# Window attention in a two-layer encoder: both halves of the 64-column values in one stationary tile, and weight splits moved to GpSimd

## The chip, the cores and the metric

The kernel runs on one core of a Trainium2 chip. The metric is the device time of one execution in microseconds (us), the median of several runs; less is better.

## What is computed

A trunk of two layers is applied to two independent groups (prompt and sample) of 512 tokens with 1024 features. Layer 0 uses latent attention with 8 heads, layer 1 uses windowed attention: 16 query heads of 64 columns share 2 key/value heads, a query block of 128 tokens sees its own and the two neighbouring key blocks, and each head adds a slope bias and a sink to its softmax. Both layers also attend into 256 memory tokens, multiply the branches by a gate, and project back. The part of the reference that the change touches is this one:

```python
def swa_mixer(q, k, v, q_norm, k_norm, sink):
    ...
    def attend(args):
        i, q_blk = args
        start = i * BLOCK
        k_blk = lax.dynamic_slice_in_dim(kp, start, 3 * BLOCK, axis=1)
        v_blk = lax.dynamic_slice_in_dim(vp, start, 3 * BLOCK, axis=1)
        ...
        s = jnp.einsum('bqkgd,bjkd->bkgqj', q_blk, k_blk).astype(jnp.float32) * scale
        s = jnp.where(valid, s - slopes * dist, NEG)
        sk = jnp.broadcast_to(sink_l, s.shape[:-1] + (1,))
        p = jax.nn.softmax(jnp.concatenate([s, sk], axis=-1), axis=-1)[..., :-1]
        return jnp.einsum('bkgqj,bjkd->bqkgd', p.astype(v_blk.dtype), v_blk)
...
branch = jnp.concatenate([mix, mem_o], axis=-1) * jax.nn.silu(gate)
x = x + branch @ p['w_out'][i]
```

## The kernel before, in words

**Precision.** Each fp32 operand of a matrix product is split into a high half (a copy in the type fp32r) and a low half (the value minus the high half, again fp32r). A product is then three matmuls: high x high, high x low, low x high (`mm3`, lines 1509 to 1511). ScalarE makes the high half with a copy, VectorE the low one with a subtraction. For weights that is `w_hi_to` (line 553) and `w_lo_to` (line 881); for a PSUM bank it is `hi` (line 560) and `lo` (lines 889 and 891). GpSimd splits only four weight tiles in the whole program (line 1368).

**Stages.** The program runs four layers in a row: L = 0 and 1 for the first group, 2 and 3 for the second. Odd L are the window layers. In one of them there are, in order: memory values and keys, projections of the tokens, memory attention, keys and values of the window part (`bKV`), queries (`bQ`), then a loop over the 16 heads, here called the window stage, and the output projection (`out`). The results of `bKV` for the values go to the tile `v0` (printed as `v` in the trace): for each key block k and each of the two value heads, 64 columns, written twice side by side, so that the 128 rows of the product hold the output in the lower and again in the upper 64 partitions; `v0[:, 0]` has the high, `v0[:, 1]` the low half.

**The loop over the heads.** Every engine has its own list of instructions, written by hand, and the engines meet at semaphores. In iteration h:

- TensorE: scores of head h+2 (`b_s`), one "fill" tile, on even h the transposes of a later query pair (`b_q`), the product with the values of head h (`b_o`), one or two more fill tiles, the transposes of the probabilities of head h+1 (`b_pt`). A fill tile is a weight row block of 256 columns from another projection (late queries, gates, parts of the output projection); `WINDOW_FILL` says how many stand before and after `b_o`.
- VectorE: low half of the weights for the first fill (`w_lo_to`), bias, row maximum of head h+2 (`b_max`, lines 1270 and 1274), low half of the queries on even h, the multiplication of `b_o`'s bank by the gate (`gated`, line 942), low halves of the weights for the second fills, sum and reciprocal of head h+2 (lines 985 and 987), low half of the transposed probabilities of head h+1 (`b_pt`, line 889). Where a chunk of fill tiles ends, its bank is also added to the residual (line 969) or to the gate (line 936) on the way.
- ScalarE: high half of the weights for the first fill, of the queries on even h, exponentials of head h+2 (lines 820 and 578), high halves of the weights for the second fills, of the transposed probabilities of head h+1, and from h = 8 on a branch split (line 591).
- GpSimd: probabilities of head h+2 times the reciprocal (line 1393, four instructions), in the first four heads the scaling of the late queries (lines 1339, 1340, 1486), and the low half of finished branches (line 1373).

The heads work two ahead, so the scores of head h+2 are computed while head h is finished. A weight tile's low half is needed by TensorE about four tiles later. PSUM has 8 banks; `plan()` hands them out ahead of time by a small model of how long each use lasts (`BANK_USE`), and a use waits until the one before it in the same bank has been read. That table's numbers set no order of the work, only which bank is taken.

`b_o` in the kernel before, for each of the four key blocks (two see 384 query columns, two 256):

```python
ins = mm3(bank(use)[:, lo_q * P:(hi_q + 1) * P],
          tuple(v0[:, a, k, c * P:(c + 1) * P] for a in range(2)),
          tuple(windowT[h % 2][:, a, SHARED_FROM[s] + col:SHARED_FROM[s] + col + span(k)]
                for a in range(2)), k == order[0], k == order[-1], skip=True)
```

## Time and profile before

| | us |
|---|---|
| median of 3 runs (lowest, highest) | 1433.49 (1433.2, 1434.6) |
| the profiled execution, its time | 1434.05 |
| the profiled execution, its span in the trace | 1432.3 |
| busy in the span: TensorE matmuls | 1393.2 (97%) |
| busy: VectorE, ScalarE, GpSimd | 981.5, 760.0, 412.8 (69%, 53%, 29%) |
| granted TensorE clock | 0.999 of full speed |

The profiled execution's own time is 0.6 us above the median of the runs and 1.75 us above its span, so times worked out on the span can be carried over to the runs by differences. The window stage takes place twice, from about 559 to 688 us and from about 1268 to 1397 us of the span. Busy shares of TensorE count overlapping matmuls as one stretch. In the rows, a name such as `w_lo_t<-w_raw,w_hi` says what an instruction writes and reads, `x2` that two instructions were merged into one row, and the bracket at a row's end how long the engine had been idle and who released it.

### The profile page before, as it was taken

Reading aid. Unit: us, or ns where it says so; the run is one execution under the profiler, and the core shown is the slowest. Engines: PE = TensorE matmul, PEld = TensorE weight load, DVE = VectorE, ACT = ScalarE, POOL = GpSimd, SP = SyncE. Lnnn points to the kernel's source line nnn. Section 1 sums busy time; section 2 is a strip of 40 time slices with the busy share of each in tenths; the row PEclk is TensorE's granted clock in tenths of the full one; section 3 lists DMA queues with packets and bytes.
Section 4 is the critical chain, followed back from the end, with each engine's and each line's share of the span. In section 5 each row is a group of like instructions: output and inputs, shape, how many; then the busy total and the mean of one; then the engine's idle time right before and its main releaser. Section 6 shows DMA issues by size and latency. Waiting matters only on the chain.

```text
span 1432.3 us, 23084 instructions
## 1 busy us (share of the span) xinstructions
PE 1393.2 (97%) x8120; PEld 1236.3 (86%) x8120; DVE 981.5 (69%) x2072; ACT 760.0 (53%) x1823; POOL 412.8 (29%) x535
## 2 busy tenths in 40 slices
PE   7999999999999999999999999999999999998999
PEld 6889889898888888798888898899888888887997
DVE  6555687887655647888664656888877556578883
ACT  7354466555544436666463535656655345366661
POOL 2231252330202223734212213422311112246450
PEclk9999999999999999999999999999999999999999
DMA  6413221114341222222262132121133413122222
GB/s 224 119 49 88 77 69 46 43 50 146 118 133 55 78 71 82 62 65 90 96 198 82 50 94 79 51 62 47 38 103 126 121 49 96 58 77 60 67 71 103
DMA packets 88674, 121.47 MB, mean 85 GB/s; under 512 B 10353, under 2 KB 58865, under 8 KB 88561
## 3 DMA queue, kind: packets, MB, share of 16 engines
q1 hardware_dynamic: 83088, 112.31, 25.9%
q10 hardware_dynamic: 5472, 7.69, 1.8%
q8 instruction: 66, 1.08, 0.3%
q14 instruction: 48, 0.39, 0.1%
HBM read 115.77 MB, written 4.19 MB: 84 GB/s over the span
## 4 chain that ended last, share of the span: by engine, by line
PE 72%; DVE 12%; ACT 9%; issue 4%; POOL 2%; ACTq 1%; DMA 0%; SPq 0%; DVEq 0%; POOLq 0%
PE bank L1509 22%; PE bank L1511 21%; PE bank L1510 21%; PE bank L1555 5%; ACT prob L578 4%; DVE bank L1270 3%; DVE w_lo_t L881 3%; DVE probT L889 2%; POOL rr L1340 1%; ACT w_hi L553 1%; PE bank L1515 1%; PE bank L1516 1%; ACT q_st L575 1%; DVE nmax L1274 1%; POOL rtmp L1339 1%
## 5 line engine op out<-in xcount | busy, mean ns | idle before, releaser
L881 DVE TENSOR_TENSOR w_lo_t<-w_raw,w_hi 128x256 fp32r<-128x256 f32 (+3 forms) x540 | 302.1, 575 | 288.4 <-ACT w_hi L553 276.0
L553 ACT ACTIVATE w_hi<-w_raw 128x256 fp32r<-128x256 f32 (+3 forms) x544 | 268.5, 509 | 334.3 <-PE bank L1511 310.2
L1509 PE MATMUL bank<-w_hi,actT 128*128 128x256 f32 (+3 forms) x1120 | 361.5, 323 | 5.5 <-DVE probT L889 3.4
L1510 PE MATMUL bank<-w_lo_t,actT 128*128 128x256 f32 (+3 forms) x1120 | 359.1, 321 | 0.0
L1509 PEld LDWEIGHTS bank<-w_hi,actT 128*128 128x128 f32 x1120 | 212.5, 190 | 21.7 <-DVE w_lo_t L881 5.6
L1510 PEld LDWEIGHTS bank<-w_lo_t,actT 128*128 128x128 f32 x1120 | 212.6, 190 | 14.3
L1393 POOL TENSOR_TENSOR prob<-prob,rinv 128x256 f32<-128x256 f32 x192 | 137.9, 748 | 283.7 <-DVE rinv L987 283.7
L1511 PE MATMUL bank<-w_hi,brlo 128*128 128x256 f32 (+1 forms) x608 | 189.0, 311 | 0.0
L578 ACT ACTIVATE prob<-bank,nmax 128x256 f32<-128x256 f32 (+2 forms) x256 | 138.3, 551 | 79.3 <-DVE nmax L1181 39.7
L1511 PE MATMUL bank<-w_hi,actT 128*128 128x512 f32 (+3 forms) x512 | 170.1, 332 | 0.0
L1509 PE MATMUL bank<-actT,w_hi 128*128 128x512 f32 x384 | 152.8, 398 | 3.9 <-DVE probT L889 2.3
L1510 PE MATMUL bank<-actT,w_hi 128*128 128x512 f32 x384 | 150.0, 391 | 0.0
L1511 PE MATMUL bank<-actT,w_lo_t 128*128 128x512 f32 x384 | 150.0, 391 | 0.0
L1339 POOL TENSOR_SCALAR rtmp<-ss 128x4 f32<-128x4 f32 (+2 forms) x84 | 25.2, 300 | 394.1 <-DVE ss L901 301.8
L1511 PEld LDWEIGHTS bank<-w_hi,brlo 128*128 128x128 f32 x608 | 115.7, 190 | 6.3
L889 DVE TENSOR_TENSOR probT<-bank,probT 128x512 fp32r<-128x512 f32 (+1 forms) x192 | 111.4, 635 | 8.3 <-ACT probT L560 7.3
L560 ACT ACTIVATE probT<-bank 128x512 fp32r<-128x512 f32 (+1 forms) x192 | 95.1, 573 | 39.2 <-PE bank L1555 39.2
L1373 POOL TENSOR_TENSOR brlo<-gate,actT 128x512 fp32r<-128x512 f32 x48 | 63.7, 1334 | 180.4 <-ACT actT L591 180.4
L1511 PEld LDWEIGHTS bank<-w_hi,actT 128*128 128x128 f32 x512 | 96.8, 189 | 7.5
L1555 PE MATMUL bank<-ident,prob 128*128 128x128 f32 x704 | 90.7, 275 | 9.1 <-ACT prob L578 6.5
L1340 POOL TENSOR_TENSOR rr<-rtmp,mhalf 128x4 f32<-128x4 f32 (+2 forms) x84 | 93.6, 1114 | 7.0
L1555 PEld LDWEIGHTS bank<-ident,prob 128*128 128x128 f32 x704 | 78.3, 140 | 18.7 <-ACT prob L578 8.6
(141 smaller groups left out, 2710.7 us busy)
## 6 DMA issues: line engine op xcount, KB each, us to landing
w_raw<-in_w_mem SPq DMA_DIRECT2D x64, 256.0 KB, 2.6
w_raw<-in_w_out SPq DMA_DIRECT2D x112, 128.0 KB, 2.1
w_raw<-in_w_b SPq DMA_DIRECT2D x112, 128.0 KB, 2.1
w_raw<-in_w_b SPq DMA_DIRECT2D x48, 256.0 KB, 2.7
w_raw<-in_w_out SPq DMA_DIRECT2D x40, 256.0 KB, 2.8
w_raw<-in_w_a SPq DMA_DIRECT2D x32, 256.0 KB, 2.7
w_raw<-in_w_a SPq DMA_DIRECT2D x64, 128.0 KB, 2.0
bias<-in_alibi ACTq DMA_DIRECT2D x28, 192.0 KB, 2.3
```

The source lines that it names most:

```text
L553: act.activation(w_hi[:, n % SPLIT, 0:width], w_raw[:, n % RAW, 0:width], ACT.Copy).then_inc(w_hi_done, 1)
L560: act.activation(out, in_, ACT.Copy, scale=1.0 if gain is None else gain).then_inc(hi_done, 1)
L578: ins = act.activation(out, in_, ACT.Exp, bias=nmax[:, par, c:c + 1], accum_out=psumx[:, par, c:c + 1])
L881: dve.tensor_tensor(w_lo_t[:, n % SPLIT, 0:width], w_raw[:, n % RAW, 0:width], w_hi[:, n % SPLIT, 0:width].bitcast(fp32), ALU.subtract).th ...
L889: ins = dve.tensor_tensor(out, in_, hi_part, ALU.subtract)
L1340: nc.gpsimd.tensor_tensor(dst, rtmp[:, 0:n], mhalf[:, 0:n], ALU.pow).then_inc(signal, 1)
L1373: nc.gpsimd.tensor_tensor(brlo[:, j, :], gate[:, j, :], actT[:, j, :].bitcast(fp32), ALU.subtract).then_inc(br_lo, 1)
L1393: pool.tensor_tensor(t, t, rinv[:, par, i:i + 1].to_broadcast(list(t.shape)), ALU.mult).then_inc(p_pool, 1)
L1509: nc.tensor.matmul(out, lhs[0], rhs[0], start=start, stop=False, skip_group_check=skip)
L1510: nc.tensor.matmul(out, lhs[0], rhs[1], start=False, stop=False, skip_group_check=skip)
L1511: return nc.tensor.matmul(out, lhs[1], rhs[0], start=False, stop=stop, skip_group_check=skip)
L1555: ins = nc.tensor.transpose(bank(use)[:, c * P:(c + 1) * P], src, ident[:])
```

## The change

**Values.** `v0[:, 0]` now holds for each value head 64 columns of the high half followed by 64 columns of the low half. The copy of ScalarE and the subtraction of VectorE write 128 x 2 x 64 elements per token block, where each wrote 128 x 256 before. `b_o` needs two matmuls per key block, with the high and with the low half of the probabilities as the moving operand, and leaves the high values' product in the lower 64 rows of the bank and the low values' product in the upper 64. A product low x low is thereby added, which was left out before.

**Adding the halves.** ScalarE copies the upper 64 rows times 0.5 to a tile `o_low` in partitions 0 to 63 (`b_low`, ahead of the exponentials of head h+2). VectorE adds the lower rows times 0.5 and writes to the lower or upper half of `o_pair` (`b_sum`, in the place of `gated`). On odd heads GpSimd multiplies the gate by the pair (`gate_pair`), after the probabilities of head h+2. The branch split of ScalarE waits for that (`o_gated`), and on even heads `b_sum` waits until GpSimd has read the pair before. Both new tiles lie where `v0[:, 1]` has no use in the window stage.

**Weight splits.** The low halves of the 256-column tiles whose place is the second fill of an iteration (`late_split`) go from VectorE to GpSimd, ahead of the probabilities of head h+2: 23 tiles in each window stage, 46 in all. Heads 0 to 3 and 6 to 10 have two such tiles each, heads 4, 5 and 11 to 13 have one.

**Planner.** `bO` counts 1.18 in place of 1.76 for its matmuls and 2.0 in place of 1.0 until it is read. This changes bank numbers; within a window stage nearly every bank is still taken over from a use of the same kind.

```diff
-            "bO": (1.76, True, 1.0, 0.7), "out": (2.7, False, 0.8, 0.65)}
+            "bO": (1.18, True, 2.0, 0.7), "out": (2.7, False, 0.8, 0.65)}
...
+                first = steps[-1][2] + SPLIT
                 fill(stream, WINDOW_FILL[h][1])
+                late_split[L, h] = (first, steps[-1][2] + SPLIT)
...
+    for part in late_split.values():
+        for n in range(*part):
+            if n < len(tiles) and tiles[n][4] == NARROW:
+                tiles[n] = tiles[n][:5] + ("pool",) + tiles[n][6:]
...
@@ ScalarE
-                    act.wait_ge(*read(use))
+                    if use[0] == "bO":
+                        act.wait_ge(o_gated, PAIRS_B * (use[1] // 2) + j + 1)
+                    else:
+                        act.wait_ge(*read(use))
...
+                        def b_low(h):
+
+                            use = ("bO", L, h)
+                            act.wait_ge(*full(use))
+                            if h > 0:
+                                act.wait_ge(*read(("bO", L, h - 1)))
+                            act.activation(o_low[half(0), :], bank(use)[half(1), :], ACT.Copy, scale=0.5).then_inc(o_low_done, 1)
...
+                            b_low(h)
                             if h + 2 < HB:
                                 b_exp(h + 2)
...
@@ VectorE
+                        def b_sum(h):
+
+                            use, n = ("bO", L, h), HB * G + h
+                            dve.wait_ge(o_low_done, n + 1)
+                            if n >= 2 and h % 2 == 0:
+                                dve.wait_ge(o_gated, n // 2)
+                            dve.scalar_tensor_tensor(out=o_pair[half(h % 2), :], in0=bank(use)[half(0), :], scalar=0.5,
+                                                     in1=o_low[half(0), :], op0=ALU.mult, op1=ALU.add).then_inc(read(use)[0], 1)
...
-                            gated(("bO", L, h), h // 2, half(h % 2))
+                            b_sum(h)
...
@@ GpSimd
+                        def gate_pair(j):
+
+                            pool.wait_ge(*read(("bO", L, 2 * j + 1)))
+                            pool.tensor_tensor(gate[:, j, :], gate[:, j, :], o_pair[:], ALU.mult).then_inc(o_gated, 1)
...
                         for h in range(HB):
                             for j in SPLIT_MEM_AT.get(h, ()):
                                 branch_lo(j)
+                            for n in range(*LATE_SPLIT[L, h]):
+                                if TILES[n][5] == "pool":
+                                    w_lo(n)
                             if h + 2 < HB:
                                 b_p(h + 2)
+                            if h % 2 == 1:
+                                gate_pair(h // 2)
...
@@ TensorE
-                                ins = mm3(bank(use)[:, lo_q * P:(hi_q + 1) * P],
-                                          tuple(v0[:, a, k, c * P:(c + 1) * P] for a in range(2)),
-                                          tuple(windowT[h % 2][:, a, SHARED_FROM[s] + col:SHARED_FROM[s] + col + span(k)]
-                                                for a in range(2)), k == order[0], k == order[-1], skip=True)
+                                for a in range(2):
+                                    ins = nc.tensor.matmul(
+                                        bank(use)[:, lo_q * P:(hi_q + 1) * P], v0[:, 0, k, c * P:(c + 1) * P],
+                                        windowT[h % 2][:, a, SHARED_FROM[s] + col:SHARED_FROM[s] + col + span(k)],
+                                        start=k == order[0] and a == 0, stop=k == order[-1] and a == 1, skip_group_check=True)
```

VectorE in head 6 of a window stage, before (`probT_69` is the transposed probabilities' second buffer, the rows `bank,mx` the bias and row maximum of the next iteration):

```order
L1274 TENSOR_SCALAR nmax<-mx,sinks 128x4
L891 SCALAR_TENSOR_TENSOR qT<-bank,gcol,qT 64x512 x2
L942 SCALAR_TENSOR_TENSOR gate<-bank,gate 64x512
L881 TENSOR_TENSOR w_lo_t<-w_raw,w_hi 128x256 x2
L985 TENSOR_TENSOR tot<-psumx,esink 128x4
L987 RECIPROCAL rinv<-tot 128x4
L889 TENSOR_TENSOR probT_69<-bank,probT_69 128x384 x2
L889 TENSOR_TENSOR probT_69<-bank,probT_69 128x512
L881 TENSOR_TENSOR w_lo_t<-w_raw,w_hi 128x256
L1270 ISA bank,mx<-bank,bias 128x384
```

The same place in the changed kernel:

```order
L1295 TENSOR_SCALAR nmax<-mx,sinks 128x4
L913 SCALAR_TENSOR_TENSOR qT<-bank,gcol,qT 64x512 x2
L1306 SCALAR_TENSOR_TENSOR o_pair<-bank,o_low 64x512
L1007 TENSOR_TENSOR tot<-psumx,esink 128x4
L1009 RECIPROCAL rinv<-tot 128x4
L911 TENSOR_TENSOR probT_71<-bank,probT_71 128x384 x2
L911 TENSOR_TENSOR probT_71<-bank,probT_71 128x512
L903 TENSOR_TENSOR w_lo_t<-w_raw,w_hi 128x256
L1291 ISA bank,mx<-bank,bias 128x384
```

The two subtractions for the second fills are gone from between the gate's place and the sum `tot`; the one for the first fill still stands between the transposed probabilities and the next row maximum.

GpSimd in heads 6 and 7, before (each head is a run of 256, 384, 384, 256 columns, the last of one merged with the first of the next):

```order
L1393 TENSOR_TENSOR prob<-prob,rinv 128x256 x2
L1393 TENSOR_TENSOR prob<-prob,rinv 128x384 x2
L1393 TENSOR_TENSOR prob<-prob,rinv 128x256 x2
L1393 TENSOR_TENSOR prob<-prob,rinv 128x384 x2
L1393 TENSOR_TENSOR prob<-prob,rinv 128x256 x2
```

And in the changed kernel:

```order
L1398 TENSOR_TENSOR w_lo_t<-w_raw,w_hi 128x256 x2
L1423 TENSOR_TENSOR prob<-prob,rinv 128x256
L1423 TENSOR_TENSOR prob<-prob,rinv 128x384 x2
L1423 TENSOR_TENSOR prob<-prob,rinv 128x256
L1398 TENSOR_TENSOR w_lo_t<-w_raw,w_hi 128x256 x2
L1423 TENSOR_TENSOR prob<-prob,rinv 128x256
L1423 TENSOR_TENSOR prob<-prob,rinv 128x384 x2
L1423 TENSOR_TENSOR prob<-prob,rinv 128x256
L1521 TENSOR_TENSOR gate<-gate,o_pair 128x512
```

Two splits now stand ahead of each head's four instructions, and the multiplication by the gate behind them on odd heads.

ScalarE in head 6, changed kernel:

```order
L564 ACTIVATE w_hi<-w_raw 128x256
L571 ACTIVATE qT<-bank,gcol 64x512 x2
L846 ACTIVATE o_low<-bank 64x512
L832 DMA bias<-in_alibi 128x384
L833 ACTIVATE esink<-nmax,sinks 128x4
L589 ACTIVATE prob,psumx<-bank,nmax 128x384 x2
L589 ACTIVATE prob,psumx<-bank,nmax 128x256 x2
L564 ACTIVATE w_hi<-w_raw 128x256 x2
L571 ACTIVATE probT_71<-bank 128x384 x2
```

Only the row `o_low` is new there; it stands ahead of the bias transfer and the exponentials of head h+2.

## Rows read from the trace of the kernel before

**Rows 1.** Page, part 1: busy time, share of the span and instructions.

```profile
PE 1393.2 (97%) x8120; PEld 1236.3 (86%) x8120; DVE 981.5 (69%) x2072; ACT 760.0 (53%) x1823; POOL 412.8 (29%) x535
```

**Rows 2.** Windows: stage of the heads, then start of the output projection.

```profile
core 0: us, PE busy (x) PEld busy (x) DVE busy (x) ACT busy (x) POOL busy (x), PEclk, DMA share, GB/s
559.00:688.00 129.00, 121.99 (x855) 113.88 (x854) 105.99 (x284) 82.21 (x241) 71.29 (x87) 1.00 0.24 74
688.00:720.00 32.00, 32.00 (x151) 26.70 (x150) 16.22 (x28) 12.92 (x25) 3.14 (x5) 1.00 0.30 94
```

**Rows 3.** Waits from 559 to 688: total us, times, longest.

```profile
ACT esink L820 <- DVE nmax L1274: 36.8, 14, 4.6
DVE w_lo_t L881 <- ACT w_hi L553: 19.9, 16, 2.4
...
PE bank L1555 <- ACT prob L578: 3.3, 4, 1.0
...
DVE probT L889 <- ACT probT L560: 0.9, 1, 0.9
```

**Rows 4.** Timeline, TensorE, product with the values: start us, duration us.

```profile
603.99 0.34 PE L1511 MATMUL bank<-probT,v 128*128 128x384 f32 x1
604.17 0.33 PE L1509 MATMUL bank<-probT,v 128*128 128x384 f32 x1
...
605.17 0.28 PE L1510 MATMUL bank<-probT,v 128*128 128x256 f32 x1
605.29 0.28 PE L1511 MATMUL bank<-probT,v 128*128 128x256 f32 x1
```

**Rows 5.** Timeline, VectorE, head 6 of the first group.

```profile
617.59 0.68 DVE L942 SCALAR_TENSOR_TENSOR gate<-bank,gate 64x512 f32<-64x512 f32 x1
619.23 0.76 DVE L881 TENSOR_TENSOR w_lo_t<-w_raw,w_hi 128x256 fp32r<-128x256 f32 x2 [0.96 <-ACT w_hi L553]
619.91 0.15 DVE L985 TENSOR_TENSOR tot<-psumx,esink 128x4 f32<-128x4 f32 x1
620.10 0.18 DVE L987 RECIPROCAL rinv<-tot 128x4 f32<-128x4 f32 x1
620.20 1.59 DVE L889 TENSOR_TENSOR probT<-bank,probT 128x384 fp32r<-128x384 f32 x3
621.70 0.42 DVE L881 TENSOR_TENSOR w_lo_t<-w_raw,w_hi 128x256 fp32r<-128x256 f32 x1
622.03 0.56 DVE L1270 CUSTOM_DVE_ANT_0 bank<-bank,bias 128x384 f32<-128x384 f32 x1
```

**Rows 6.** Timeline, ScalarE, same head.

```profile
618.77 0.73 ACT L553 ACTIVATE w_hi<-w_raw 128x256 fp32r<-128x256 f32 x2
619.39 1.37 ACT L560 ACTIVATE probT<-bank 128x384 fp32r<-128x384 f32 x3
```

**Rows 7.** Timeline, GpSimd, same head.

```profile
620.36 3.02 POOL L1393 TENSOR_TENSOR prob<-prob,rinv 128x256 f32<-128x256 f32 x4 [6.77 <-DVE rinv L987]
```

**Rows 8.** Source and tile views: minimum, median and maximum duration in ns.

```profile
L1368 POOL TENSOR_TENSOR w_lo_t<-w_raw,w_hi x4: 1272/1298/1299, 10.7 to 1091.9; 128x512 fp32r<-128x512 f32 x4
...
L560 ACT ACTIVATE krT<-bank x32: 579/588/597, 191.2 to 1033.2; 64x512 fp32r<-64x512 f32 x32
```

**Rows 9.** Timeline: VectorE subtractions that meet a GpSimd instruction, and that instruction.

```profile
576.50 0.98 DVE L881 TENSOR_TENSOR w_lo_t<-w_raw,w_hi 128x256 fp32r<-128x256 f32 x1
601.08 1.21 DVE L881 TENSOR_TENSOR w_lo_t<-w_raw,w_hi 128x256 fp32r<-128x256 f32 x1 [0.96 <-ACT w_hi L553]
...
575.01 2.94 POOL L1393 TENSOR_TENSOR prob<-prob,rinv 128x256 f32<-128x256 f32 x4 [1.76 <-DVE rinv L987]
599.48 2.54 POOL L1373 TENSOR_TENSOR brlo<-gate,actT 128x512 fp32r<-128x512 f32 x2
```

**Rows 10.** Timeline, VectorE, head 14: the gate's place and what follows.

```profile
682.23 0.67 DVE L942 SCALAR_TENSOR_TENSOR gate<-bank,gate 64x512 f32<-64x512 f32 x1
682.83 0.67 DVE L881 TENSOR_TENSOR w_lo_t<-w_raw,w_hi 128x512 fp32r<-128x512 f32 x1
684.42 1.62 DVE L889 TENSOR_TENSOR probT<-bank,probT 128x384 fp32r<-128x384 f32 x3 [0.92 <-ACT probT L560]
```

**Rows 11.** Timeline, GpSimd, probabilities of the last head, then the next instruction.

```profile
679.58 3.21 POOL L1393 TENSOR_TENSOR prob<-prob,rinv 128x256 f32<-128x256 f32 x4 [3.52 <-DVE rinv L987]
682.74 1.90 POOL L1373 TENSOR_TENSOR brlo<-gate,actT 128x512 fp32r<-128x512 f32 x1
```

More of the change, by code:

```diff
@@ L937, in gate_tile, with gated @@
                                                           op0=ALU.add, op1=ALU.mult).then_inc(read(use)[0], 1)
-                def gated(use, j, rows=slice(0, P)):
+                def gated(use, j):
                     dve.wait_ge(*full(use))
-                    dve.scalar_tensor_tensor(out=gate[rows, j, :], in0=bank(use)[rows, :], scalar=0.5,
-                                                          in1=gate[rows, j, :], op0=ALU.mult, op1=ALU.mult).then_inc(read(use)[0], 1)
+                    dve.scalar_tensor_tensor(out=gate[:, j, :], in0=bank(use)[:], scalar=0.5,
+                                                          in1=gate[:, j, :], op0=ALU.mult, op1=ALU.mult).then_inc(read(use)[0], 1)
                 def chunk_end():
```

27 lines of the change are left out of this document (15 added, 12 removed).

## Prediction, on record before the changed kernel ran

> **What bounds the kernel now.** The page's busy shares come first: TensorE 97%, VectorE 69% [rows 1]. That invites the reading that a matmul removed is time won. It holds where TensorE has no gap, as in the output projection (32.00 us busy of 32.00), and less in the stage that the change touches, where TensorE is busy 121.99 of 129 us [rows 2]. So I asked the waits of that stage who waits for whom [rows 3]. The reader is to look for one thing there: does anything on VectorE wait for TensorE? Nothing does. VectorE waits 19.9 us for ScalarE's high halves of weights and 0.9 us for those of the probabilities, and that is all; it is busy 106 us, which with these waits fills the stage. ScalarE waits 36.8 us, nearly all of its pause, for VectorE's row maximum. TensorE waits little, but what it waits for are exponentials and splits.
>
> So VectorE and ScalarE form a closed loop, once round per head: row maximum, exponentials, weight splits, sum and reciprocal, split of the transposed probabilities, split for the first fill, next row maximum. TensorE runs beside it, with 7 us of gaps per stage. This stage ends with the loop, and each part of the change is worth what it does to the loop.
>
> **TensorE's part.** Per head 12 matmuls become 8. One with 384 columns follows the other at 0.18 us, one with 256 at 0.12 us (differences of starts) [rows 4]. Two of each go: 0.6 us per head, 32 heads, 19 us of work. By the above it goes into waiting: bound from below 0, from above 19 us. I take 0, except at the stage's end.
>
> **ScalarE's part.** The new copy of 64x512 should take about the 0.59 us of the copy of the same shape to krT [rows 8]. It stands where ScalarE waits for the row maximum, 36.8/14 = 2.6 us on average [rows 3]; 16 x 0.59 = 9.4 us fit. Without that cover it would delay the exponentials by up to 0.6 us; that is the case if `b_o` ends late, and TensorE now ends it 0.6 us earlier. Price 0.
>
> **VectorE's part.** `b_sum` reads a bank and one SBUF tile and writes 64x512, as the 0.68 us multiplication did [rows 5]: 0. The values' split shrinks from 256 to 128 elements in 8 instructions outside the loop: 0. What matters is the second fills' subtractions. In head 6 the exponentials end shortly before 618.9 (the next copy starts at 618.77 [rows 6]); call 618.9 E. Before, VectorE waits 0.96 us for the first high half, subtracts twice (0.76), sums, inverts, and starts on the probabilities at 620.20, that is E+1.3 [rows 5]. Without the subtractions the reciprocal is ready by about E+0.4, but the next instruction needs ScalarE's high half of the probabilities, which still comes behind two weight copies: started 619.39, three in 1.37 us, so the first is done about 619.9 [rows 6]. VectorE then starts at E+1.0. **The subtractions taken away, 0.76 us, shorten the loop by 0.3.** This also shows what is late next.
>
> **GpSimd's part.** A split of 128x512 takes 1.30 us there [rows 8], so one of 128x256 about 0.65. The two start when the high half is there, 0.42 us into ScalarE's pair, about 619.25, and end at 620.55. The four probability instructions started at 620.36 and took 3.02 us [rows 7]; they now start 0.2 us later. TensorE reads them a head later, so that alone costs nothing.
>
> **Where the two meet.** The subtraction for the first fill stays on VectorE, between the probabilities and the next row maximum. When it meets a GpSimd instruction it is long: 1.21 us at 601.08, ending at 602.29, which is 0.27 us after the pair `brlo` ended at 602.02; and 0.98 at 576.50 within the probabilities [rows 9]; alone it takes 0.42. In head 6 it started at 621.70 [rows 5], just where the second of the four ends (half of 3.02 us after 620.36, about 621.8): it lost almost nothing. In the changed kernel VectorE is there 0.3 us earlier, at 621.4, and the second instruction ends 0.2 us later, at about 622.0; the subtraction would end 0.27 us after that, 622.25, where before it ended at 622.12. **So the loop gets back to its row maximum 0.1 us later, not 0.3 us earlier.**
>
> The Trainium skill says the same as a rule in "SBUF — State Buffer", section "Who interferes with whom": a VectorE instruction with two SBUF inputs contends with a GpSimd instruction that reads SBUF, and the one that comes second waits for the whole of the other. By the rule, work moved to GpSimd is not free for VectorE; the rows of 601.08 and 576.50 agree. Without it the sum would be the second rival's.
>
> **The sum for one stage**, head by head by the same working (gains positive, in us):
> - Two splits, plain (heads 0, 6, 7, 9, 10): -0.1 each, -0.5.
> - Head 1: its subtraction lost 0.56 to the lock before [rows 9]; it now meets the second instruction instead of the third: +0.6.
> - Head 4: the 1.21 us subtraction leaves VectorE [rows 9], of which the high halves let 0.9 count, but the next one meets `brlo` and loses about 0.5: +0.4.
> - Head 8 adds two finished banks between its two splits, so ScalarE is ahead and most of the 0.76 goes: +0.5. Head 2 is like it with the gate, but one split hides behind ScalarE: +0.2. In head 3 the subtraction waits for ScalarE's copy, then meets GpSimd's third instruction, which is 0.2 later: -0.2.
> - One split (5, 11, 12, 13): half the delay on GpSimd, together +0.1.
> - The end: `b_sum` of head 14 waits for GpSimd's multiplication, which stands behind the last head's probabilities (end 682.79 [rows 11]) and takes about the 1.3 us of such an instruction, so 684.1 against 682.23; behind it are a subtraction of 0.67, which may meet GpSimd's next, and the last probabilities (684.42 before) [rows 10]. That is 1.1 to 1.6 us late, less the 0.6 us that the last `b_o` is shorter: -0.5.
>
> Together +0.6 per stage, 1.2 in all; each term is good to 0.2 us, so with 30 heads the sum is good to some 5. Row 7 of the last output rows comes 2 us later, but is read fourth, after three rows of 12 matmuls at 32.00/151 = 0.21 us, 2.5 us each [rows 2], and its own chain before took about 3 us: 0. Bank numbers in the later layers: 1 us either way. From the profiled 1434.05 this gives 1432.9, from the median 1433.49 **1432.3 us**.
>
> **The rivals.**
> 1. *TensorE is the bound after all.* For it: 97% busy, 122 of 129 us in the stage [rows 1, 2]. Against: no wait of VectorE for it. All 19 us come: 1414.8. Chance 0.10.
> 2. *The loop shortens by what the high halves allow*, since GpSimd's instructions leave gaps into which the subtraction slips. For it: in head 6 the subtraction lost almost nothing before [rows 5]. 13 heads x 0.3 = 3.9, 0.9 more from heads 4 and 8, per stage 4.8, both 9.6 us: 1424. Decides from: less than 0.1 us lost to GpSimd per head. Chance 0.27.
> 3. *Slower: GpSimd's splits are longer than half of 1.30 us.* At 0.85 us each (the instruction's fixed part not halved) the second probability instruction ends 0.4 us later, the first fill's subtraction with it, in 9 heads of a stage, and 0.2 in 5 heads: 4.6 us, less the 0.6 above, twice 4: 1441.5; with 0.75 us half of it, 1437. It decides from 0.70 us on. For it: the four probability instructions average 0.75 us at 320 columns [rows 7], more per column than the 1.30 at 512. Chance 0.21.
>
> That the change does not remove the work is ruled out by the lists: 8 rows in place of 12.
>
> **How the numbers follow.** A measurement of this kernel can tell about 0.2% from no change, 2.9 us. My forecast, chance 0.42, is 1428.5 to 1436.5, mostly within that: 0.36 no change, 0.04 faster, 0.02 slower. Rival 1 and 2 are faster (0.37), rival 3 slower (0.18) or the same (0.03). Faster 0.41, same 0.39, slower 0.20. The range takes in rival 2 and the middle of rival 3: 1420 to 1438; without them it would be 1428.5 to 1436.5.
>
> **What would show it.** In the new profile: TensorE idle in the stage up from 7 to some 16 us, its new waits on VectorE's and ScalarE's probabilities; the stage still about 129 us; the first fills' subtractions at 0.6 to 0.9 us in place of 0.42; VectorE waiting for ScalarE's `probT` in every head; `o_low` always ready when `b_sum` comes, except in head 14. Wrong if the stage gets shorter by more than 3 us, or if VectorE starts to wait for `o_low`, which would put TensorE into the loop.

## The result, and the profile after

| | before | changed |
|---|---|---|
| median of 9 runs each, us | 1433.50 | 1437.57 (1436.33 to 1440.6) |
| ratio, 95% interval | | 1.0028 (1.0018 to 1.0038) |
| span of the profiled execution, us | 1432.3 | 1434.5 |
| first sink exponential to end of the last value product, stage 1, 2 | 141.52, 141.70 | 143.13, 143.12 |

The kernel became 4.1 us slower (the interval of the ratio lies above 1); 1432.3 us was forecast, 1.2 less than before and not to be told from no change. The profiled execution of the changed kernel is its fastest run. At 52 us it is 1.1 us ahead of the one before: its first weight product starts 0.37 us sooner (12.07 against 12.44), and the kernel before then had a granted TensorE clock of 0.50 from 13.5 to 17.0 us, which the changed one had not. So its span shows less of the loss than the median does.

The page of the changed kernel, span and part 1, answers to [rows 1]:

```profile
span 1434.5 us, 22921 instructions
...
PE 1379.3 (96%) x7992; PEld 1216.1 (85%) x7992; DVE 975.0 (68%) x2026; ACT 778.4 (54%) x1855; POOL 462.9 (32%) x597
```

The windows, as [rows 2]:

```profile
559.00:688.00 129.00, 113.89 (x781) 102.58 (x780) 102.29 (x258) 90.32 (x253) 93.98 (x115) 1.00 0.23 73
688.00:720.00 32.00, 31.29 (x147) 25.80 (x146) 16.25 (x28) 13.06 (x25) 4.41 (x6) 1.00 0.28 91
```

TensorE has 8 us less to do in the stage and is idle for 15 us where it was idle for 7: its saving went into waiting, as forecast. VectorE has 3.7 us less to do, and the stage still got longer. The second window is new: the output projection, which had no gap, now has one of 0.7 us.

The waits from 558 to 688 us, as [rows 3] (a row's three numbers are total us, times, longest):

```profile
POOL w_lo_t L1398 <- ACT w_hi L564: 32.6, 13, 4.2
ACT esink L833 <- DVE nmax L1295: 20.4, 14, 2.3
DVE tot L1007 <- ACT prob L589: 16.8, 12, 2.4
ACT o_low L846 <- PE bank L1890: 11.6, 9, 2.4
...
DVE probT L911 <- ACT probT L571: 3.1, 7, 0.5
```

The 19.9 us in which VectorE waited for high halves of weights became 16.8 us for the exponentials themselves: the closed loop of VectorE and ScalarE is still there, and VectorE still waits for nothing of TensorE's. So the question is what made a round of the loop longer. The starts of two successive sink exponentials (`esink`) measure one round. Head h of the prediction lies between the exponentials of heads h+2 and h+3. Stage 1, in us; a gain is positive:

| head | before | changed | gain | forecast |
|---|---|---|---|---|
| 0 | 8.19 | 8.43 | -0.24 | -0.1 |
| 1 | 8.76 | 8.88 | -0.12 | +0.6 |
| 2 | 9.54 | 9.43 | +0.11 | +0.2 |
| 3 | 8.76 | 9.20 | -0.44 | -0.2 |
| 4 | 9.10 | 8.47 | +0.63 | +0.4 |
| 5 | 9.05 | 9.07 | -0.02 | see 11 |
| 6 | 8.19 | 8.41 | -0.22 | -0.1 |
| 7 | 8.04 | 8.86 | **-0.82** | -0.1 |
| 8 | 9.84 | 8.87 | +0.97 | +0.5 |
| 9 | 9.39 | 10.12 | **-0.73** | -0.1 |
| 10 | 8.65 | 8.84 | -0.19 | -0.1 |
| 11, 12 | 7.79, 7.79 | 7.87, 7.86 | -0.15 | +0.1 with head 5 |
| the end | 11.71 | 12.10 | -0.39 | -0.5 |

The sum is -1.6 where +0.6 was forecast. Heads 1, 7 and 9 hold 2.1 of the 2.2 us between them. Head 7, VectorE's timeline in the changed kernel:

```profile
628.68 0.89 DVE L903 TENSOR_TENSOR w_lo_t<-w_raw,w_hi 128x256 fp32r<-128x256 f32 x1
...
631.25 0.13 DVE L1291 DVE_READ_ACCUMULATOR2_ANT mx<- 128x1 f32 x1
631.42 0.68 DVE L1295 TENSOR_SCALAR nmax<-mx,sinks 128x4 f32<-128x4 f32 x1
```

and GpSimd's there:

```profile
626.50 1.43 POOL L1398 TENSOR_TENSOR w_lo_t<-w_raw,w_hi 128x256 fp32r<-128x256 f32 x2 [4.08 <-ACT w_hi L564]
627.90 2.93 POOL L1423 TENSOR_TENSOR prob<-prob,rinv 128x256 f32<-128x256 f32 x4
630.79 1.28 POOL L1521 TENSOR_TENSOR gate<-gate,o_pair 128x512 f32<-128x512 f32 x1
```

The first fill's subtraction takes 0.89 us where [rows 5] had 0.42, as forecast. What the prediction had not seen is the line below it. The negated row maximum `nmax`, four columns wide, takes 0.68 us, where it takes 0.23 when alone, and it ends at 632.10, just as GpSimd's new gate multiplication does (632.07). ScalarE's exponentials wait for exactly this instruction. All 14 of a stage, in the source view from 558 us on: minimum, median and maximum in ns.

```profile
L1295 DVE TENSOR_SCALAR nmax<-mx,sinks x14: 228/442/1167, 561.1 to 675.4; 128x4 f32<-128x4 f32 x14
```

Over a stage `nmax` loses 3.65 us in this way (its durations less 0.23); in the kernel before it lost 2.3, in five heads, to GpSimd's branch splits `brlo`. The Trainium skill, "SBUF — State Buffer", section "Who interferes with whom", names both groups that can meet the SBUF port lock that VectorE and GpSimd share: VectorE instructions with two SBUF inputs, which the prediction used, and `copy`, `cast` and `tensor_scalar` where their operands allow a 2-port mode, which it passed over. The rows above are of the second group.

At the stage's end TensorE starts to wait where it never did. ScalarE's timeline:

```profile
688.22 0.59 ACT L846 ACTIVATE o_low<-bank 64x512 f32<-64x512 f32 x1 [2.33 <-PE bank L1890]
690.93 0.63 ACT L605 ACTIVATE actT<-gate 128x512 fp32r<-128x512 f32 x1 [2.12 <-POOL gate L1521]
```

Behind this wait of 2.12 us stand, in ScalarE's list, the squares of the next memory rows. Their factor reaches VectorE late (it waits 3.3 us for it, 2.0 before), and behind VectorE's row norm stand the weight splits. TensorE's weight loads, waits from 684 to 704 us; before there were none:

```profile
PEld bank L1549 <- DVE w_lo_t L903: 1.1, 1, 1.1
```

Against the kernel before, TensorE's instructions fall back here by 1.0 us, of which 0.35 is made good at 746 us.

### The profile page after: what moved, and what is told of

Its sections match the earlier page's. It is cut to its first block, busy times and chain, and to the rows that moved or that the text cites. A ratio compares the mean times of both kernels' runs of the same rounds, so it can differ in the third digit from the quotient of the medians.

```text
span 1434.5 us, 22921 instructions
## 1 busy us (share of the span) xinstructions
PE 1379.3 (96%) x7992; PEld 1216.1 (85%) x7992; DVE 975.0 (68%) x2026; ACT 778.4 (54%) x1855; POOL 462.9 (32%) x597
## 3 DMA queue, kind: packets, MB, share of 16 engines
q8 instruction: 65, 1.06, 0.3%
## 4 chain that ended last, share of the span: by engine, by line
PE 67%; DVE 14%; ACT 10%; issue 4%; POOL 3%; ACTq 1%; DMA 0%; SPq 0%; DVEq 0%; POOLq 0%
PE bank L1549 20%; PE bank L1551 20%; PE bank L1550 20%; PE bank L1595 5%; ACT prob L589 4%; DVE bank L1291 4%; DVE w_lo_t L903 3%; DVE probT L911 2%; ACT w_hi L564 2%; POOL rr L1370 1%; ACT probT L571 1%; DVE nmax L1295 1%; PE bank L1555 1%; PE bank L1556 1%; ACT q_st L586 1%
## 5 line engine op out<-in xcount | busy, mean ns | idle before, releaser
L903 DVE TENSOR_TENSOR w_lo_t<-w_raw,w_hi 128x256 fp32r<-128x256 f32 (+3 forms) x494 | 286.6, 595 | 249.8 <-ACT w_hi L564 237.5
```

The source lines that it names most:

```text
L903: dve.tensor_tensor(w_lo_t[:, n % SPLIT, 0:width], w_raw[:, n % RAW, 0:width], w_hi[:, n % SPLIT, 0:width].bitcast(fp32), ALU.subtract).th ...
```

## Which part costs: the splits or the packing

**e1: the 46 splits back on VectorE** (the packing alone), **e2: the kernel before with only the splits on GpSimd.**

```diff
-                tiles[n] = tiles[n][:5] + ("pool",) + tiles[n][6:]
+                tiles[n] = tiles[n][:5] + ("dve",) + tiles[n][6:]
```

> The changed kernel with the 46 second-fill splits back on VectorE; the packed values, the copy, the sum and GpSimd's gate multiplication stay. Loop theory (VectorE and ScalarE set the pace of the window stage, and GpSimd's splits push the four probability instructions into VectorE's own split): the loop gets its old pace back, the row of exponentials of successive heads falls on the old distances, and what is left over the kernel before is the end of a stage (about 0.4 us each) and, once, the copies that queue on ScalarE behind its wait for GpSimd's last gate multiplication (1.0 us): 1433.5 + 1.8 = 1435.3 us, 1434.3 to 1436.3. Rival (the chain copy, sum, gate across three engines is what costs): no better than the changed kernel, 1437.6. Rival (TensorE's saving counts once VectorE is not disturbed): 1415 to 1425.

> The kernel before with nothing but the 46 second-fill splits moved to GpSimd, three matmuls per key block as before. Loop theory: the splits for the first fills on VectorE take 0.6 to 0.9 us in place of 0.42 in most heads, as in the changed kernel, the loop is 1.2 us longer in each stage: 1433.5 + 2.4 = 1435.9 us, 1434.9 to 1437. Rival (the chain of the halves costs, the splits do not): 1433.5 or below, down to 1428, since VectorE has 35 us less to do.

Measured: e1 1441.04 us against 1434.41 (ratio 1.0050, 1.0037 to 1.0064), e2 1431.92 (0.9984, 0.9976 to 0.9993). Both expectations of the loop theory fell: e1 came 5.7 us above its value, and for e2 it had the wrong sign. The splits on GpSimd gain 2.5 us, the packing costs 6.6, and 6.6 - 2.5 is the 4.1 of the change. In e1 another two-input instruction is the victim, the sum of head 4; VectorE's timeline, then GpSimd's:

```profile
601.20 1.24 DVE L1007 TENSOR_TENSOR tot<-psumx,esink 128x4 f32<-128x4 f32 x1
...
599.70 2.73 POOL L1403 TENSOR_TENSOR brlo<-gate,actT 128x512 fp32r<-128x512 f32 x2
```

`tot` takes 0.15 us when alone. Head 4's round is 10.19 us in e1, 9.10 before.

**e3: a third matmul per key block, back into the changed kernel** (the product of the low probabilities is made twice, so that it counts double in the output).

```diff
-                                for a in range(2):
+                                for n, a in enumerate((0, 1, 1)):
```

> The changed kernel with a third matmul per key block, the pass of the low probabilities done twice (so that low product is counted twice in the output). This gives TensorE back the whole 19 us. Loop theory: that work runs in TensorE's gaps; only the last product of each stage is 0.6 us longer: 1437.6 to 1438.9 us. Rival (TensorE bounds the stage, and something else ate the saving): 1450 or more.

Measured: 1439.59 us (1.0043, 1.0031 to 1.0056): 2.0 us above the changed kernel by the medians, 1.1 if each is taken against the kernel before of its own series. The stages are 143.58 and 143.57 us, 0.45 more, of which 0.3 is the end. So the 19 us of TensorE's work are worth 1 to 2 us, where the rival needed 12 or more. TensorE is not the bound.

**e4: GpSimd's splits behind the probabilities**, not ahead of them.

> The changed kernel with GpSimd's splits behind the four probability instructions in place of ahead of them. Loop theory: the probabilities start when the reciprocal is ready, about 1.1 us earlier against the exponentials; VectorE's split for the first fill then comes near the end of the third of them (estimate from its own rows: it is wanted 2.6 us after the exponentials, the third ends at 2.7) and ends at 3.0 in place of 3.5: 0.4 to 0.5 us per head in some 26 heads, 11 us: 1426.5 us, 1423 to 1431. Rival (ScalarE's high halves set VectorE's pace, the meeting with GpSimd does not): 1437.6. Rival (a split that comes later on GpSimd stops TensorE): above 1438.

Measured: 1442.70 us (1.0057, 1.0044 to 1.0069), so the expectation was wrong by 16 us. It had looked only at the first fill's subtraction, which did get shorter (its excess per stage fell from 4.6 to 3.2 us). GpSimd's queue now ended later, and the row maximum met it more often. `nmax` and GpSimd's queue in head 7:

```profile
632.67 1.29 DVE L1295 TENSOR_SCALAR nmax<-mx,sinks 128x4 f32<-128x4 f32 x1
...
631.26 1.43 POOL L1398 TENSOR_TENSOR w_lo_t<-w_raw,w_hi 128x256 fp32r<-128x256 f32 x2
632.65 1.29 POOL L1521 TENSOR_TENSOR gate<-gate,o_pair 128x512 f32<-128x512 f32 x1
```

The excess of `nmax` is 7.1 us per stage here, against 3.65. This is what made the row maximum the new suspect.

## Taking the collision away, from either side

**f1: all gate multiplications on VectorE; f2: only the last two of a stage.**

```diff
+                            if h % 2 == 1:
+                                dve.wait_ge(*read(("bO", L, h)))
+                                dve.tensor_tensor(gate[:, h // 2, :], gate[:, h // 2, :], o_pair[:], ALU.mult).then_inc(o_gated, 1)
```

> The changed kernel with all 16 gate multiplications of each window layer on VectorE, right behind the sum of the pair, in place of GpSimd. Collision theory: the packing costs its time because GpSimd's gate multiplication stands where VectorE writes the next negated row maximum (0.68 us in place of 0.23 in every second head, and the exponentials wait for it), because the sum of head 14 waits for it, and because ScalarE stands 2.1 us before the last one. All three go: 0.45 us in some 5 heads and 0.4 at the end of each stage, 1.0 once: 5 to 6 us less than the changed kernel, 1431.5 to 1433; VectorE's own multiplication (0.6 us) fits where it waits 0.8 to 2.4 us for the exponentials. Rival (the cost of the packing is ScalarE's copy and the later splits of the values, not GpSimd's multiplication): no less than the changed kernel, 1437 to 1440, since VectorE gets 0.6 us more per pair.

> The changed kernel with only the last two gate multiplications of each window layer (heads 13 and 15) on VectorE. Collision theory: the end of each stage is 0.4 us shorter, ScalarE no longer waits at the end of the stage and the delay of 1.0 us behind it in the first group goes; the distances between the exponentials of heads 2 to 13 stay as they are. 1.8 to 2.8 us less than the changed kernel: 1434.8 to 1435.8. Rival: the wait at the end is hidden behind the output projection, 1437.5.

Measured: f1 1434.81 us against 1434.56 (1.0001, 0.9992 to 1.0010), f2 1435.74 (1.0009, 1.0000 to 1.0018). Both are faster than the changed kernel by the medians: f2 by 1.8 us, at the edge of what was expected, f1 by 2.8, half of it. (With each taken against the kernel before of its own series the gains are 2.9 and 3.8.) In f1 the rounds of heads 7 and 9 fell to 8.42 and 9.19, as they should. But head 4 rose from 8.47 to 9.01: GpSimd's branch split moved up into the place of its multiplication, under the next row maximum (0.68 us). Head 11 rose from 7.87 to 8.35 for another reason; its row maximum takes 0.23 us there. A stretch of lower TensorE clock stands in it, which is taken up below. The same holds for f2's profiled execution, one of its slowest (1437.62 us), with four such stretches: its stage 1 is 143.86 us, no shorter, since head 11 takes 8.29 us there and the end 12.35. In stage 2, where no such stretch stands at the end, the end is 10.87 against 12.11, the gain that was looked for, but head 11 takes 9.04. The wait in front of the output projection fell from 1.1 to 0.5 us, which shows the chain behind ScalarE's wait. How much of f2's gain in the median each part gives, this one trace cannot tell.

**f3: the changed kernel with another form of the row maximum; f4: the kernel before with the same.** The sink becomes the start of the maximum, and the negation a `tensor_reduce` over one element:

```diff
-                                                                   scale=1.0, scalar=-3.0e38, op0=ALU.add, op1=ALU.max,
+                                                                   scale=1.0, scalar=sinks[:, h:h + 1], op0=ALU.add, op1=ALU.max,
...
-                            dve.tensor_scalar(nmax[:, h % 2, :], mx[:, h % 2, :], sinks[:, h:h + 1], -1.0, ALU.max, ALU.mult).then_inc(max_ready, 1)
+                            dve.tensor_reduce(nmax[:, h % 2, :], mx[:, h % 2, :].unsqueeze(2), AX, ALU.max, negate=True).then_inc(max_ready, 1)
```

> The changed kernel; the negated row maximum of 128x4 is a reduction over one element with negation in place of a tensor_scalar with maximum and multiplication, the sink goes in as the start of the maximum. Collision theory, if the tensor_scalar is held up by GpSimd because it reads SBUF through two ports: it takes 0.25 us or less in every head, with GpSimd's multiplication beside it, the odd heads' distances fall by up to 0.45 us, 3.65 us per stage in all where nothing else is late next, and half to all of it counts: 1431 to 1434. Rival (any VectorE instruction that reads or writes SBUF there is held up): it stays at 0.68 beside GpSimd's multiplication and the time at 1437.5.

> The kernel before with the same form of the negated row maximum. Collision theory: it was held up 5 times per stage by GpSimd's splits of the gated tiles, 2.3 us per stage in all; half to all of it goes: 2.3 to 4.6 us less than the kernel before, 1429.5 to 1432. Rival: unchanged durations and 1434.

Measured: f3 1433.07 us against 1434.56 (0.9990, 0.9982 to 0.9999), f4 1431.32 (0.9975, 0.9966 to 0.9985). By the medians f3 is 4.5 us below the changed kernel (5.6 with each against its own series), and f4 is 3.2 below the kernel before. Source view of f3, the 14 of a stage:

```profile
L1295 DVE TENSOR_REDUCE nmax<-mx x14: 156/157/160, 561.5 to 674.0; 128x4 f32<-128x4 f32 x14
```

and what stands beside the one in head 7, VectorE and then GpSimd:

```profile
631.74 0.16 DVE L1295 TENSOR_REDUCE nmax<-mx 128x4 f32<-128x4 f32 x1
...
630.99 1.29 POOL L1521 TENSOR_TENSOR gate<-gate,o_pair 128x512 f32<-128x512 f32 x1
```

The reduction lies in the middle of the same GpSimd instruction and takes 0.16 us. The rival, that any small VectorE instruction is held up there, is out. The Trainium skill says in the same section of "SBUF — State Buffer" that on trn2 a `tensor_reduce` never contends, since it has no 2-port mode. These 14 rows agree. That the two ports are the reason is the page's statement: the runs show only that the one form waits and the other does not. So the held row maximum is shown to be a part of the loss. It is not the whole, because f4 gains too: with the new form the change still costs 1433.07 - 1431.32 = 1.8 us. And each form was changed together with the sink's way into the maximum, which by the source view adds 0.02 to 0.03 us to each of the four instructions before it; that works against the gain.

## What is left of the packing's cost

> The changed kernel with all gate multiplications on VectorE and the one-port form of the negated row maximum. Collision theory: what the gate on VectorE gave back, since GpSimd's splits of gated tiles moved up under the next row maximum (distances 6 to 7, 10 to 11, 12 to 13, 13 to 14), is gone too; the stage is 140.0 us or less from the exponentials of head 0 to the end of the last value product, against 143.1 of the changed kernel and 141.0 of the one-port form alone, 1430 to 1432. Rival (beyond the row maximum the VectorE time of the 8 multiplications counts): 1433 or more, as with the one-port form alone.

> The kernel before with only the 46 splits on GpSimd and the one-port form of the row maximum: the candidate to beat both. If the gains of the two are separate (2.5 and 3.2 us), 1428.5 to 1429. If the same collision stood behind both, no more than the better of the two: 1431.3.

> The changed kernel with the 46 splits back on VectorE and the one-port form of the row maximum, so the packing alone, without the collisions of the row maximum. With the old row maximum the packing alone cost 6.6 us over the kernel before. Collision theory: against the kernel before with the one-port form (1431.3) it now costs 2 us or less, 1431 to 1433.5. Rival (the packing's cost is ScalarE's copy in the loop and the order of the splits): it still costs 5 us or more, 1436 or more.

Measured against 1433.86: **g1** 1431.97 us (0.9989, 0.9980 to 0.9998), **g2** 1429.22 (0.9966, 0.9954 to 0.9978), **g3** 1435.28 (1.0013, 1.0004 to 1.0022). g1's stages are 141.40 and 140.53 us, no shorter than f3's 141.00 and 140.33, so the expectation for the stage fell, though the time lies within its range (1.9 us under the kernel before, where f3 is 1.5 under it). Its head 11 (8.27 and 8.50 us) and its end in stage 1 (12.34, 11.30 in stage 2) are long in the same way as f2's. g2 comes out near the sum of two gains: it beats both kernels. g3 lies between its theories: the packing alone still costs 4.6 us with the row maximum free (gap to the kernel before +1.4, f4's -3.2). The largest single piece of that is head 4, 9.73 us against f4's 8.64: `tot` is held there for 1.24 us, as in e1.

So I laid g2 and f3 side by side, which differ in the packing alone. In the odd heads of either stage, and in head 12, f3 is 0.13 to 0.17 us longer (one round of head 11 apart), in the even heads not, and the end is 0.64 longer. In head 1, where I compared them, VectorE's durations are the same. The place is on ScalarE. f3, after `o_low`:

```profile
630.70 0.60 ACT L846 ACTIVATE o_low<-bank 64x512 f32<-64x512 f32 x1
...
632.31 0.30 ACT L833 ACTIVATE esink<-nmax,sinks 128x4 f32<-128x4 f32 x1 [1.01 <-DVE nmax L1295]
632.63 0.58 ACT L589 ACTIVATE prob<-bank,nmax 128x384 f32<-128x384 f32 x1
```

The first exponential starts 0.32 us after the sink's. In all 32 heads of the kernel before it is 0.32 where ScalarE's last instruction was the queries' copy with 64 partitions (14 heads, 0, 2, 4 and so on to 12), and 0.20 where it was one with 128 (18 heads). `b_low`, with 64 partitions, stands ahead of the exponentials of heads 2 to 15. So the packing brings the longer distance to the rounds that had the short one, seven per stage, and leaves the others as they were.

**h1: the copy over all 128 partitions of the bank**, on top of f3. The sum then adds the high values' product to itself and leaves out the low values':

```diff
-                            act.activation(o_low[half(0), :], bank(use)[half(1), :], ACT.Copy, scale=0.5).then_inc(o_low_done, 1)
+                            act.activation(o_low[:], bank(use)[:], ACT.Copy, scale=0.5).then_inc(o_low_done, 1)
```

> The changed kernel with the one-port row maximum, where ScalarE's copy for the sum takes all 128 partitions of the bank in place of the lower half's 64 (the sum then adds the wrong half, so the output differs). In all traces so far the first exponential starts 0.20 us after the sink's where ScalarE's instruction before has 128 partitions, and 0.32 where it has 64 (the queries' copy, and now the copy of 64x512). If the number of partitions decides: 0.20 in heads 2 to 15, the distances from an odd head to the next even one fall by 0.12 to 0.14 (7 per stage), the end by 0.1: some 2 us less than the 64-partition form (1433.1), 1431. If any further instruction there does it: 0.32 and 1433.

Measured: 1428.57 us against 1434.17 (0.9964, 0.9952 to 0.9976), more than expected. **i1** is the same with the sum reading partitions 64 to 127 of the copy (`in1=o_low[half(1), :]`), so that both products are added again; **i2** has this copy and sum, and the row maximum as it was.

> The changed kernel with the one-port row maximum and ScalarE's copy over all 128 partitions; the sum adds partitions 64 to 127 of the copy, so the computation is the whole one again. If the gain of the 128-partition copy (4.5 us against the 64-partition form) comes from the number of partitions alone: 1428 to 1429, and 5 us below the kernel before. If the sum's two halves at different partitions cost VectorE something: its 0.68 us gets longer, and the time 1430 or more.

> The changed kernel, its row maximum as it was, with ScalarE's copy over all 128 partitions alone. What is open: how much of the change's 4.1 us comes from the 64-partition copy, where GpSimd still holds up the row maximum. If both costs stand beside each other in the loop: 2 x (13 x 0.13) = 3.4 us less than the changed kernel, 1434. If what is won in front of the exponentials runs into GpSimd's instructions again (a row maximum ends with them, wherever it starts): less than 1.5 us of it, 1436 to 1437.5.

Measured against 1434.19: i1 1428.85 us (0.9960, 0.9948 to 0.9973), i2 1435.38 (1.0009, 1.0000 to 1.0018). i1 at the same place:

```profile
629.90 0.60 ACT L846 ACTIVATE o_low<-bank 128x512 f32<-128x512 f32 x1
...
631.50 0.30 ACT L833 ACTIVATE esink<-nmax,sinks 128x4 f32<-128x4 f32 x1 [1.00 <-DVE nmax L1295]
631.70 0.56 ACT L589 ACTIVATE prob<-bank,nmax 128x384 f32<-128x384 f32 x1
```

0.20 us in all of heads 2 to 15, with a copy just as long (0.60). The stage is 138.42 and 138.40 us, against 141.00 and 140.33 in f3: 13 rounds by 0.14 are 1.8 us. The 0.7 more of stage 1 is one round of head 11 (8.19 in f3, 7.33 in i1) that was long in f3's first stage alone. i2 is 2.2 us faster than the changed kernel by the medians (2.9 with each against its own series), between its two expectations: each round but head 4's is 0.11 to 0.16 shorter, as if both costs stood beside each other, except head 11 of stage 1, where `nmax` meets `brlo` and takes 1.15 us (8.90 in place of 7.87; in stage 2 it is 7.73).

**What made single rounds long: TensorE's clock.** f3, stage 1: the window from 661 to 664 us, then TensorE's timeline.

```profile
661.00:664.00 3.00, 3.00 (x14) 3.00 (x14) 2.55 (x7) 2.38 (x6) 2.62 (x4) 0.50 0.14 44
...
659.57 1.36 PE L1595 MATMUL bank<-ident,prob 128*128 128x128 f32 x10 [2.11 <-ACT prob L589]
...
661.38 0.52 PE L1555 MATMUL bank<-krT,qT 128*128 128x384 f32 x1
661.70 0.52 PE L1556 MATMUL bank<-krT,qT 128*128 128x384 f32 x1
```

Behind a pause of 2.11 us the granted clock fell to 0.50, the level of 1.2 GHz, from 660.7 to 664.1, and a matmul of 384 columns followed the other at 0.32 us where it is 0.18 at full clock. In stage 2 the same pause (2.10 us) had no such stretch behind it. The copy `o_low` of head 11 in stage 1, then in stage 2:

```profile
666.22 0.60 ACT L846 ACTIVATE o_low<-bank 64x512 f32<-64x512 f32 x1 [2.85 <-PE bank L1890]
...
1373.63 0.60 ACT L846 ACTIVATE o_low<-bank 64x512 f32<-64x512 f32 x1 [1.33 <-PE bank L1890]
```

In stage 1 the product came late, the row maximum had already ended at 665.97, and the exponentials stood behind the copy: 0.7 us (8.19 against 7.48). This is the case that the prediction named under ScalarE's part ("if `b_o` ends late") and priced at 0. In i2 the slow stretch (659.9 to 663.3) acts by another way: it delays a transposed block, so that VectorE's subtraction starts 0.05 us after GpSimd's third probability instruction in place of 0.02 before it, takes 1.06 us in place of 0.43, and the row maximum behind it meets `brlo`. A stretch in head 4 (f3, 599.3 to 602.7) cost nothing: 8.45 us, 8.47 in stage 2.

All 12 kernels with the packing have this lower clock in most executions: 93 of their 101 list a granted clock of 0.993 to 0.999. Of the 26 executions of e2, f4 and g2, which keep the third matmul, none does. In the traces, the packed kernels have pauses of TensorE of 1.6 to 2.6 us in the stage, the others none above 1.5. So a part of the packing's cost in the medians can be the clock's. How large it is in the changed kernel is not shown: its profiled execution had no slow stretch, and at 1436.33 us it is 1.2 below its median and 2.8 above the kernel before.

Medians less the kernel before of the same series, in us:

| | no packing | packing, copy of 64 | packing, copy of 128 |
|---|---|---|---|
| row maximum as it was, splits on VectorE | 0 | +6.6 | |
| the same, splits on GpSimd | -2.5 | **+4.1** | +1.2 |
| `tensor_reduce`, splits on VectorE | -3.2 | +1.4 | |
| the same, splits on GpSimd | -4.6 | -1.5 | **-5.3** |

The last row, from left to right: with the row maximum free, the packing costs 3.1 us, and with the wide copy it gains 0.7, which the intervals can't tell from nothing. So with the splits on GpSimd 3.5 of the packing's 6.6 us go with the collisions of the row maximum (6.6 less 3.1), and 3.8 with the wide copy. The shares depend on the order: taken away first, the copy gives 2.9; and with the splits on VectorE the row maximum takes only 2.0 (6.6 less 4.6).

The 3.8 us are not all a cost of the packing: the wide copy also shortens the even heads, in which the kernel before had the 0.32 from its queries' copy. By the traces (f3 less g2, stage 2, without a slow stretch), the packing's 1.6 us with the row maximum free are 1.05 in seven rounds through the copy and 0.64 at the end, less 0.1 in head 4. i1 still loses 0.5 at the end against g2, and gets 0.8 back in the even heads.

## Why the prediction was wrong, point by point

The forecast of 1432.3 us had the wrong sign: the kernel became slower. That 1437.6 still lies just inside the range of 1420 to 1438 is owed to rival 3, for which the range was widened, and rival 3's reason did not hold.

- **"VectorE and ScalarE form a closed loop", TensorE's part at 0**: right in the main. Idle time rose from 7 to 15 us in the stage as forecast, and e3 puts the 19 us at 1 to 2. Rival 1 is out. But "bound from below 0" is not safe: with the longer pauses came stretches of half clock, and one of them cost 0.7 us in f3.
- **"ScalarE's part ... Price 0"** is the first step that failed. The copy's 0.59 us was hidden, as argued: VectorE waits for `o_low` only in the last head of each stage. But the copy also changes what ScalarE did last before the exponentials: 0.13 us more in each of seven rounds per stage that had an instruction of 128 partitions there, some 1.8 us in all. (Widening it gives more, 2.9 us with the row maximum as it was and 3.8 with it free, since it also helps the rounds that had 0.32 before.) The rows for it stood in the trace before, in the odd heads beside the even ones; the prediction priced durations alone.
- **"Where the two meet"** is the second. It asked of one VectorE instruction, the first fill's subtraction, whether it meets GpSimd. It is right about that one: 0.90 us in head 6, next maximum 3.50 us after ScalarE's second-fill copy starts, against 3.26 before; the loop got 0.24 later, not 0.1. But the gate multiplication, 1.3 us more on GpSimd in every odd head, was priced only at the stage's end. In heads 1, 7 and 9 it, or the branch split pushed back by it, holds the row maximum for 0.46 to 0.94 us. For head 7 the runs give each term: 8.04 before, 0.24 by the splits (e2: 8.28), 0.46 by the row maximum, 0.13 by the copy, together 8.87; measured 8.86. Heads 1 and 9 come out in the same way: 8.27 in e2, 0.46 and 0.13, together 8.86 (8.88 measured), and 9.06 in e2, 0.94 and 0.13, together 10.13 (10.12 measured). So the +0.6 of head 1 was near what the splits alone give (0.49), and the packing took it away.
- **"so one of 128x256 about 0.65"**: 0.72 to 0.74 us. The point from which rival 3 decides (0.70) was passed, and its time for 0.75 us, 1437, is what came. But its reason is not the cause: e2 has the same splits on GpSimd and gains 2.5 us. That its time came was luck.
- **Heads 4 and 8**: the gains of 0.4 and 0.5 came as 0.63 and 0.97. In e2, which has the splits alone, head 8 gives 0.95, and heads 1 and 9 give 0.49 and 0.33; with the losses in other heads 1.1 us are left of it in stage 1. Head 4 gives only 0.06 there, since `brlo` holds its row maximum (0.69 us); in the changed kernel GpSimd is later and the row maximum takes 0.23. So head 8's term was too low by half, and head 4's 0.63 takes both parts of the change.
- **"The end ... -0.5"**: -0.39. `b_sum` of head 14 waits 1.81 us for GpSimd's multiplication and starts at 684.16, where 684.1 was forecast; the loop's 1.2 us of delay and the execution's earlier start cancel in that number.
- **"Row 7 ... 0"**: failed. The row itself was in time. What stands behind ScalarE's wait for it was not: memory rows, their factor, VectorE's norm, weight splits, 1.0 us on TensorE. f1, f2 and g1, with the last gate on VectorE, have 0.35 to 0.38 there, e2 and f4 none.

## What to carry to other kernels

Before work goes to GpSimd, list every VectorE instruction in the window where it will run that has two SBUF inputs or is a `tensor_scalar` from SBUF to SBUF, however small, and ask which other engine waits for it: a four-column instruction was held for up to 1.07 us here (1.30 in e4, 0.23 alone). A reduction with negation in its place made both kernels faster, by 3.2 and 4.5 us. When an instruction is put into an idle stretch, look at what the next one does behind it, not only at whether its own time fits. And when work is taken from TensorE in a stage that it does not bound, look at the granted clock of every execution: the longer pauses can bring it down.

## What the runs showed of the hardware

- A ScalarE instruction of 64 partitions ahead of a pair of 128-partition instructions made the second of the pair start 0.12 us later (0.32 in place of 0.20), though ScalarE had been idle for 0.5 to 2.2 us between them in the kernel before. Widening it to 128 partitions removed that in all 28 heads from 2 to 15 of h1, i1 and i2, at the same duration (0.60 us). Other numbers of partitions were not tried. I had not expected that a hidden instruction costs anything.
- The collisions are not a matter of chance. In stage 1 of the kernel before, the changed one and f1, `nmax` is held 16 times, and 15 times it starts 0.62 or 0.63 us after GpSimd's instruction of 128x512 has started. The subtraction for the first fill sets this phase, since both engines are held by it. Head 8 before, VectorE and then GpSimd (each row read alone, with a narrow window):

```profile
639.13 0.42 DVE L881 TENSOR_TENSOR w_lo_t<-w_raw,w_hi 128x256 fp32r<-128x256 f32 x1
641.40 0.68 DVE L1274 TENSOR_SCALAR nmax<-mx,sinks 128x4 f32<-128x4 f32 x1
...
639.15 1.09 POOL L1393 TENSOR_TENSOR prob<-prob,rinv 128x384 f32<-128x384 f32 x1
640.77 1.29 POOL L1373 TENSOR_TENSOR brlo<-gate,actT 128x512 fp32r<-128x512 f32 x1
```

GpSimd's instruction of 384 columns takes 0.83 us alone; here it comes second, takes 1.09, and ends 0.69 us after the subtraction. One more of 256 columns, and `brlo` starts 1.22 us after the subtraction's end. VectorE's row maximum starts 1.85 us after that end, in all 28 heads of both kernels' first stages. 1.85 less 1.22 is the 0.63. So the first meeting of the two engines brings about the second: whatever GpSimd has next behind the probabilities lies under the row maximum.

- TensorE's granted clock fell to 0.50 (1.2 GHz) for 3.4 us behind a pause of about 2 us in f3's stage 1, and did not behind the same pause in its stage 2. What decides it is not shown.
- The queue of ScalarE issues the bias transfer between the row maximum and the sink's exponential: in f3 `nmax` ends at 631.90 and `esink` starts at 632.31, 0.41 us later; in the last two heads, which have no transfer, it starts 0.03 us later (675.67 and 675.70 in i2). So a round has 0.38 us of it. Moving it was not tried.
